# RWKV scan: the products of a tile's inversion and of its neighbour's recurrence issued alternately, head by head

## The reference, cut to what matters

```python
def step(S, inp):
    w_t, k_t, v_t, kk_t, a_t = inp[:5]
    S = (S * w_t[:, :, None, :]
         - jnp.einsum('bhvk,bhk->bhv', S, kk_t)[..., None] * (kk_t * a_t)[:, :, None, :]
         + v_t[..., None] * k_t[:, :, None, :])
    y = jnp.einsum('bhvk,bhk->bhv', S, inp[5]) if emit else None
    return S, y
```

## Time and profile before

| | |
|---|---|
| median of 3 runs | 4022.08 us (4013.43 to 4032.09) |
| the profiled execution | 4017.63 us |
| its span, first to last instruction | 4015.8 us |
| mean granted clock of TensorE | 0.979 of full speed |
| the RWKV scan in it | from about 515 to 870 us |

### The profile page before, as it was taken

One profiled execution on the slowest core, in us unless ns is written; L12 is line 12 of the kernel. 1 busy time (PEld: TensorE's weight loads), 2 busy tenths in 40 slices (PEclk: granted clock), 3 DMA queues, 4 the chain that ended last, 5 costly groups with the idle time before them and its releaser, 6 DMA issues.

```text
span 4015.8 us, 70971 instructions
## 1 busy us (share of the span) xinstructions
PE 3828.5 (95%) x30814; PEld 3144.7 (78%) x30814; DVE 2085.2 (52%) x2908; ACT 1308.6 (33%) x1889; POOL 145.3 (4%) x195
## 2 busy tenths in 40 slices
PE   7998968989999999999989999999999988999998
PEld 5766868888868888888877688887888877688887
DVE  4977566755454445334755553354333755553335
ACT  4244233313333233222423522223222332532222
POOL 0000012230000000000000000000000000000000
PEclk8999979999999999999999999999999999999999
DMA  6213000023343223333102033323333201033331
GB/s 249 73 53 116 11 3 3 4 83 132 126 142 105 95 95 95 105 95 105 59 3 88 11 110 97 103 89 100 95 96 109 65 13 66 24 94 101 95 105 53
DMA packets 317735, 327.81 MB, mean 82 GB/s; under 512 B 8016, under 2 KB 241504, under 8 KB 316016
## 3 DMA queue, kind: packets, MB, share of 16 engines
q1 hardware_dynamic: 310064, 286.87, 21.9%
q0 software_dynamic: 7360, 36.40, 2.5%
HBM read 314.86 MB, written 8.39 MB: 80 GB/s over the span
## 4 chain that ended last, share of the span: by engine, by line
PE 84%; DVE 9%; ACT 3%; issue 2%; DMA 1%; POOL 0%; DVEq 0%; ACTq 0%; SPq 0%
PE psum L247 83%; DVE arena L301 2%; PE psum L254 2%; ACT arena L351 1%; DVE arena L312 1%; DVE ring L332 1%; DVE r L301 1%; DVE ring L301 1%; ACT r L351 1%; ACT ring L351 1%; DMA ring<-in_w_ada 0%; DVE arena L332 0%; DMA ring<-in_w_in 0%; DVE arena L316 0%; DVE ring L308 0%
## 5 line engine op out<-in xcount | busy, mean ns | idle before, releaser
L247 PE MATMUL psum<-r 128*128 128x512 f32 (+2 forms) x12912 | 2830.5, 380 | 31.4 <-DVE r L301 29.2
L247 PEld LDWEIGHTS psum<-r 128*128 128x128 f32 x12912 | 2334.6, 188 | 499.3 <-DVE r L301 30.4
L301 DVE TENSOR_TENSOR r<-ring,r 128x2048 fp32r<-128x2048 f32 (+1 forms) x259 | 573.2, 2213 | 309.9 <-ACT r L351 306.3
L351 ACT ACTIVATE r<-ring 128x2048 fp32r<-128x2048 f32 (+1 forms) x259 | 478.2, 1846 | 366.5 <-PE psum L247 310.5
L351 ACT ACTIVATE arena<-psum 128x512 f32<-128x512 f32 (+6 forms) x505 | 265.7, 527 | 978.1 <-PE psum L247 905.1
L247 PE MATMUL psum<-arena 64*64 64x64 f32 (+10 forms) x5922 | 453.7, 261 | 30.3 <-DVE arena L301 10.8
L247 PEld LDWEIGHTS psum<-arena 64*64 64x64 f32 (+5 forms) x5922 | 313.3, 151 | 154.7 <-issue 87.6
L301 DVE TENSOR_TENSOR arena<-arena,psum 128x512 f32<-128x512 f32 (+4 forms) x209 | 130.9, 626 | 569.6 <-PE psum L247 551.8
L247 PE MATMUL psum<-ring 64*64 64x64 f32 (+3 forms) x7792 | 291.0, 229 | 41.3 <-ACT ring L351 16.7
L247 PEld LDWEIGHTS psum<-ring 64*64 64x64 f32 (+2 forms) x7792 | 251.2, 139 | 64.7 <-issue 28.6
L351 ACT ACTIVATE r<-arena 128x512 fp32r<-128x512 f32 (+1 forms) x176 | 109.4, 622 | 503.0 <-DVE arena L301 500.8
(11 more groups left out here) (114 smaller groups left out, 1487.3 us busy)
## 6 DMA issues: line engine op xcount, KB each, us to landing
ring<-in_ffa_w_in SPq DMA_DIRECT2D x88, 512.0 KB, 4.7
ring<-in_ffb_w_in SPq DMA_DIRECT2D x88, 512.0 KB, 4.6
ring<-in_w_mlp SPq DMA_DIRECT2D x32, 1024.0 KB, 5.0
ring<-in_w_in SPq DMA_DIRECT2D x31, 1024.0 KB, 5.1
ring<-in_w_ada SPq DMA_DIRECT2D x24, 1024.0 KB, 5.0
ring<-in_mix_w_in SPq DMA_DIRECT2D x24, 1024.0 KB, 4.9
ring<-in_ffa_w_out SPq DMA_DIRECT2D x20, 1024.0 KB, 4.9
ring<-in_ffb_w_out SPq DMA_DIRECT2D x20, 1024.0 KB, 4.8
```

Of the source, the lines that this page charges most:

```text
L247: ins = self.raw.matmul(o, l, r, start=start, stop=stop, skip_group_check=True)
L301: self.done(self.raw and self.raw.tensor_tensor(o, a, b, f), keys)
L351: self.done(self.raw and self.raw.activation(o, i, f, scale=scale, bias=bias), keys)
```

## The change

The generators of stages 1 and 2 give a `yield False` after each head's products (after each of the four products of the state, and each group of y, too), and a `yield True` where a turn ends. `side_by_side` draws one piece from each of the two stages in turn until both have come to their `yield True`; the inversion's piece comes first. Then the operands stage goes on by one turn as before. `in_turns` lets the gated delta rule see only the ends of turns, so its order stays. The programs of the other engines are not touched. A stage's waits still stand ahead of its first piece of the turn, so those of the recurrence now come behind the inversion's first head.

```diff
--- before.py
+++ after.py
@@ -1960,6 +1960,20 @@
             for o, other, l, r, key in products:
                 t.mm(o[HALF[1 - p if other else p], c], l[HALF[p], c], r[HALF[p], c], True, True,
                      *([key] if h == 7 and p == 1 else []))
+        yield False
+
+
+def in_turns(steps):
+
+    for last in steps:
+        if last:
+            yield
+
+
+def side_by_side(*streams):
+
+    while streams:
+        streams = [s for s in streams if not next(s)]
 
 
 
@@ -1980,15 +1994,15 @@
     for n in range(1, 6):
         o = t.take(st, "X", n, key)
         t.wait_ge(*(K.at(*ready) if n == 1 else K.at(st, "T", n - 1, key)))
-        pe_blocks(t, (o, True, s.AT, s.T, (st, "X", n, key)))
-        yield
+        yield from pe_blocks(t, (o, True, s.AT, s.T, (st, "X", n, key)))
+        yield True
         o = [t.take(st, "N", n, j, key) for j in range(2 if n < 5 else 1)]
         t.wait_ge(*K.at(st, "Xs", n, key))
         both = [(o[0], False, s.X, s.TT, (st, "N", n, 0, key))]
         if n < 5:
             both.append((o[1], True, s.TT, s.X, (st, "N", n, 1, key)))
-        pe_blocks(t, *both)
-        yield
+        yield from pe_blocks(t, *both)
+        yield True
 
 
 def act_invert(a, K, st, s, low, key):
@@ -2396,7 +2415,13 @@
 
 
 def pe_rwkv(E, K):
-    rw_turns([(pe_rw_operands(E, K, d), pe_rw_inverse(E, K, d), pe_rw_recur(E, K, d)) for d in range(2)], IN_TURN)
+    parts = [(pe_rw_operands(E, K, d), pe_rw_inverse(E, K, d), pe_rw_recur(E, K, d)) for d in range(2)]
+    for turn in range(TURNS * 8 + TURNS // 2):
+        for d in range(2):
+            tile, i = divmod(turn - TURNS // 2 * d, TURNS)
+            side_by_side(*[parts[d][k] for k in (1, 2) if 0 <= tile - k < 6 and (k < 2 or i < 6)])
+            if 0 <= tile < 6:
+                next(parts[d][0])
 
 
 def act_rwkv(E, K):
@@ -3289,7 +3314,7 @@
         o = t.take(st, "kb", l, ti)
         for f in range(4):
             t.tr(o[:, 128 * f:128 * f + 128], m.qk[:, 4 + f, 128 * ti:128 * ti + 128], *([(st, "kb", l, ti)] if f == 3 else []))
-        yield from pe_invert(t, K, st, s, (l, ti), (st, "TT0", l, ti))
+        yield from in_turns(pe_invert(t, K, st, s, (l, ti), (st, "TT0", l, ti)))
         o, o2 = t.take(st, "U0", l, ti), [t.take(st, "W", l, ti, p) for p in (0, 1)]
         t.wait_ge(*K.at(st, "T", 5, (l, ti)))
         t.wait_ge(*K.at(st, "kb sb", l, ti))
```

## The result

The changed kernel takes 4116.26 us (median of four runs, 4112.56 to 4119.32), the kernel before on the same chip 4023.94 (four runs, 4013.43 to 4032.09): a ratio of 1.0224, 95% interval 1.0211 to 1.0237. That is 92 us more; 54 were forecast, and the end of the range, 4098, is passed by 18. The profiled execution took 4117.87 us.

A forecast was written before the change was run, and what follows sets the result against it. TensorE's own time was taken as the bound, busy 95% of 4015.8 us. Shape changes 48.8, gains -6, moved waits 12.5, shrinking early waits -3 and clock +2 summed to 54 us: 4074 us, range 4042 to 4098.

The forecast's parts named there:

- The price of a change of shape: TensorE, x and s turns: each stay in a shape costs 0.142 or 0.190 us extra; 324 more changes, 48.8 us.
- Which products share the array: TensorE quadrants: only direction 1 gains, AK behind X1 (2.3 us) and u behind X3 (3.7 us), together 6 us.
- The moved waits: Waits before x of direction 1, X1 of direction 0 and K transposes grow: 3.1 us a tile, 12.5 in four tiles.
- The clock falls: Rival: longer TensorE waits lower the granted clock in up to eight places, +30 to +60 us, 4105 to 4135; chance 0.07.
- waits of 2.4 us: Clock rival's size for TensorE's longer waits, which would reach a fallen clock in up to eight places.
- The term for the clock: From 600 to 640 us, granted clock 0.79, a slot costs twice; a tenth or so of extra work there: +2 us.
- the argument's own bound: Against the falling clock: TensorE waits up to 1.9 us after 640 us left the clock at 1.00.
- The sum: Whole change: 48.8 - 6 + 12.5 - 3 + 2 = 54 us more, 4074 us, 1.3% slower.

The follow-up runs named there:

- e_shape: Kernel before, with each state product of the x turn followed by two heads of AK, nothing else touched: 4049.87 us.
- e_shape2: Kernel before, with state and AK products alternating in x turns, and s and y alternating product by product in latent tiles: 4063.69 us.
- e_64: Changed kernel with only 64x64 products alternating; x state products, s and y go as one piece behind the inversion's first head: 4063.86 us.
- d_wait: Kernel before, with ScalarE's last copy of A for direction 0 made five more times in tiles 1 to 5, delaying X1: 4058.14 us.
- after_fill: Changed kernel with needless products of constants ahead of all its long TensorE waits behind 600 us: 4088.18 us.
- p_u: Changed kernel's alternation in the u turns alone, all other turns in the order of the kernel before: 4035.88 us against 4025.94.
- before_fill: Kernel before, with needless products ahead of seven TensorE waits between 515 and 630 us: 4011.47 us against 4021.46.
- d_fill: Changed kernel with 40 needless 64x64 products ahead of the wait of X1 of direction 0 in tiles 1 to 5: 4103.73 us.
- p_x: Changed kernel's alternation in the x turns alone, all other turns in the order of the kernel before: 4073.79 us against 4025.94.
- shape2_wait: Kernel before, with x and s turns of the recurrence alternating shapes and five needless ScalarE copies before X1 of direction 0: 4097.34 us.
- p_u_fill: Alternation in the u turns alone, plus needless products ahead of seven waits between 515 and 630 us: 4023.35 us.
- before_fill2: Kernel before, with needless products ahead of seven waits between 515 and 630 us, longer in the first waits: 4011.47 us against 4022.61.

## Why the prediction was wrong

By its own steps:

**The price of a change of shape: right.** Rounds of 0.68 with s and 0.86 with y (0.67 and 0.85 forecast). For x, the row at 708.83 holds four rounds of ten instructions with an N head; in the trace they start at 708.83, 709.43, 710.07 and 710.71, 0.61 to 0.64 apart (0.62). The work added is 37.9, and 7.4 is gained, so 45.3 for 324 changes, 0.140 each; forecast 48.8. e_shape and e_shape2 give 0.127 and 0.136 without any alternation of two stages.

**Which products share the array: right, with a misread row.** "Starts 30 in 0.80 us", 60 and 13 are the counts in brackets, of instructions that ran in the stretch, those begun ahead of it included; 27, 54 and 11 start in it. With a slot of 0.058 us that is one instruction a slot in each quadrant all the same, and 0.058 is what the sums used. X3 and u of direction 1 were to fall from 1.90 to 1.15:

```profile
793.97 1.16 PE L247 MATMUL psum<-arena 64*64 64x64 f32 x48
```

e_64 puts all such gains at 7.4 us of work. By the Trainium skill (TensorE: Matmul & The Clock Gate, Part 3, "What overlaps and what doesn't") matmuls keep program order in start and end, strictly. By that rule a head of X with one u would take three slots; with the 0.058 of a slot that is 24 x 0.058 + 0.22 = 1.6 us, an estimate. The trace disagrees: 1.16.

**The moved waits: right in place, and in size where they came.** x of direction 1 waits 1.35 to 1.62 (1.47 forecast), X1 of direction 0 2.5 to 2.8 in three places and hardly in a fourth (2.5), the K transposes 1.7 and 1.8 in two places (1.9 to 2.2), but only 0.3 and 0.4 in the two others. Their sum was forecast too high (+9.5, it is +6.3).

**"The clock falls": the step that failed.** It stood among the rivals with 0.07 and 4105 to 4135, and that is what happened. Against it the forecast set that waits up to 1.9 us after 640 us had left the clock at 1.00. But it had itself worked out waits of 2.4 us in up to eight places, and the only wait of that size before, 2.9 us, stood beside a clock of 0.79. The row that bore on the question was the near one, and it was overruled by rows of shorter waits. It was not alone, either. Waits of the kernel before from 515 to 560 and from 560 to 640 us, and the table:

```profile
PE psum L247 <- ACT ring L351: 6.2, 2, 5.6
PE psum L247 <- ACT arena L351: 2.9, 1, 2.9
```

```profile
PE psum L247 <- DVE ring L332: 5.8, 2, 3.9
PE psum L247 <- ACT ring L351: 4.3, 2, 3.3
```

```profile
515.00:600.00 85.00, 64.30 (x1698) 59.90 (x1691) 55.14 (x94) 30.28 (x69) 11.05 (x16) 0.80 0.01 3
```

With the one at 602 us these are five waits of 2.9 to 5.6 us, and in the trace the clock falls in each of them or within 0.6 us behind (at 519.0, 542.9, 559.9, 573.6 and 600.9 us, for 3.4 to 17.1 us). "Waits of 2.4 us" lay between five that all had a fall and the 1.9 us that had none. The term for the clock was +2 and measures +48.3. d_wait shows the mechanism with no change of order, after_fill shows it undone, and p_u shows that even the argument's own bound was no bound: 1.76 us was enough in two places of four. Nor was the kernel before itself as whole as the one profile that the argument used: before_fill, whose products from 640 us on stand in the old order, has a fall of 3.4 us at 753.8, behind a wait of 1.4.

**The sum.** +92.5 in the scan against +54: clock +46 over the forecast, waits -3, work -5.

**What stays open**: what about the time around a wait decides. In one place waits of 1.6 us lower the clock (d_fill), and in another 2.7 us do not (p_u, at 628 us); p_x has falls behind waits of 0.96 and 0.92 us (at 651.7 and 788.3), where x alternates ahead of them. And one and the same kernel varies in it from execution to execution. In the 18 profiled executions every fall from 600 us on to the scan's end begins in a wait of TensorE or at most 2.6 us behind one of some 0.6 us or more; needless products in the waits prevent most of them; and next to changes of shape they seem to last longer. The runs don't show by what measure.

## What to carry to other kernels

Alternating two independent streams product by product saved work here only where both had one shape and lay in different quadrants, and even that was lost, since a loop ended right behind: the time won became waiting (p_u). Group by shape: each change cost 0.14 us here, more than a 64x64 product takes in its quadrant (two slots, 0.117). Before lengthening any wait of a busy TensorE, look at every wait of about that length in the trace, also outside the stretch that the change touches, and whether the clock falls at it; if so, price the stretch behind it at twice its work. Where such waits can't be removed, try to fill them. And look at the granted clock of several executions: one profile can be one of the better ones.

## What the runs showed of the hardware that was not expected

- A wait of 3.1 us in an otherwise full stretch put TensorE at 1.2 GHz for 3.4 or 13.7 us (d_wait). With products that alternate in shape around it the stretches were 6.8 to 20.5 us long (shape2_wait), and 13.7 to 23.9 at the waits of 2.5 to 2.8 us in the changed kernel.
- Waits of 1.76 us were followed by it, or had it begin in them, in five places of eight, waits of 1.0 in none of twelve (p_u and p_u_fill; before, before_fill and before_fill2).
- The kernel before spreads over 28 us (4014.62 to 4042.25), and its granted clock (0.980 to 0.973) accounts for all of it.
- Needless products made the kernel faster: 326 of them in the scan, two instructions each, made it 4011.47 us instead of 4022.61, ratio 0.9967 (0.9954 to 0.9979; before_fill2).
